# Linear-attention values as 512-column products by token tile, placed first among the side products

## The reference

```
h = RMSNorm(x);  P = h @ w_in
A = sparse attention(P): compressed blocks, selected blocks, sliding window
B = gated linear attention(P): q_b, k_b (256 columns each), v_b (512 columns), r_b, decay gate
x += (sigmoid(gA) * (A @ w_pa) + sigmoid(gB) * (B @ w_pb)) @ w_out
x += (gelu(dwconv3(h2 @ w_u)) * (h2 @ w_g)) @ w_down,   h2 = RMSNorm(x)
```

## Time and profile before

| | us |
|---|---|
| median of 3 runs (2158.03 to 2160.08) | 2159.13 |
| the profiled execution, its own time | 2148.94 |
| its span, first to last instruction | 2147.2 |
| PE busy | 2107.1 (98%) |
| DVE busy | 1144.9 (53%) |

### The profile page before, as it was taken

One profiled execution on the slowest core, in us unless ns is written; L12 is line 12 of the kernel. 1 busy time (PEld: TensorE's weight loads), 2 busy tenths in 40 slices (PEclk: granted clock), 3 DMA queues, 4 the chain that ended last, 5 costly groups with the idle time before them and its releaser, 6 DMA issues.

```text
span 2147.2 us, 30516 instructions
## 1 busy us (share of the span) xinstructions
PE 2107.1 (98%) x11911; PEld 1687.4 (79%) x11911; DVE 1144.9 (53%) x2384; ACT 516.2 (24%) x1108; POOL 675.8 (31%) x789
## 2 busy tenths in 40 slices
PE   8999989999999999999999999999999999999999
PEld 7787866678888888888887877666788888888887
DVE  5566746755337455453336666567453454555522
ACT  3124124532112222210122232244221222222000
POOL 5240042204223444434331400621232234444332
PEclk9999999999999999999999999999999999999999
DMA  5874631113222222222284736201132222222222
GB/s 155 273 236 181 248 118 40 41 43 101 79 82 79 79 79 89 90 79 74 68 291 120 267 136 273 81 28 32 59 104 82 79 79 79 79 89 91 79 69 75
DMA packets 172305, 237.53 MB, mean 111 GB/s; under 512 B 39551, under 2 KB 151680, under 8 KB 169408
## 3 DMA queue, kind: packets, MB, share of 16 engines
q1 hardware_dynamic: 153320, 133.11, 20.6%
q0 software_dynamic: 18400, 102.36, 12.8%
q10 hardware_dynamic: 444, 0.12, 0.0%
HBM read 222.76 MB, written 21.11 MB: 114 GB/s over the span
## 4 chain that ended last, share of the span: by engine, by line
PE 91%; DVE 2%; ACT 2%; POOL 2%; DMA 2%; issue 1%; SPq 0%; POOLq 0%; DVEq 0%; ACTq 0%
PE PS L1005 52%; PE PS L948 10%; PE PS L1163 6%; PE PS L970 5%; PE PS L996 3%; PE PS L1499 2%; PE PS L1416 2%; PE PS L460 2%; PE PS L1427 2%; DMA arena<-in_cache_kv_slc_dram,idx 2%; ACT arena L1710 1%; POOL arena L835 1%; PE PS L1374 1%; PE PS L1399 1%; PE PS L1548 1%
## 5 line engine op out<-in xcount | busy, mean ns | idle before, releaser
L1005 PE MATMUL PS<-arena,ring 128*128 128x272 f32 x1632 | 401.3, 393 | 0.9 <-DVE xT L2076 0.6
L1005 PEld LDWEIGHTS PS<-arena,ring 128*128 128x128 f32 x1632 | 309.3, 190 | 65.9 <-issue 2.4
L1710 ACT ACTIVATE arena<-PS 128x272 f32<-128x272 f32 (+12 forms) x442 | 176.1, 423 | 739.6 <-PE PS L1005 286.4
L2076 DVE TENSOR_TENSOR arena<-PS,arena 128x272 f32<-128x272 f32 (+4 forms) x298 | 138.7, 476 | 370.8 <-PE PS L1005 279.4
L1005 PE MATMUL PS<-hT,ring 128*128 128x272 f32 x1120 | 282.3, 397 | 5.9 <-DVE arena L2076 4.7
L1005 PEld LDWEIGHTS PS<-hT,ring 128*128 128x128 f32 x1120 | 213.6, 192 | 52.8 <-DVE arena L2076 5.2
L2076 DVE TENSOR_TENSOR xT<-PS,xT 128x272 f32<-128x272 f32 x224 | 99.0, 442 | 252.2 <-PE PS L1005 251.9
L862 POOL TENSOR_TENSOR qT<-ring 128x512 f32<-128x512 f32 (+1 forms) x38 | 48.8, 1284 | 384.7 <-PE PS L1005 255.7
L2082 DVE SCALAR_TENSOR_TENSOR arena<-arena,prm 128x32 f32<-128x32 f32 (+1 forms) x176 | 143.8, 817 | 22.1 <-ACT arena L1710 18.2
L948 PE MATMUL PS<-hT,ring 128*128 128x272 f32 x640 | 150.7, 394 | 2.3 <-DVE small L2373 1.5
L1005 PE MATMUL PS<-arena,kv_kT 128*128 128x272 f32 x616 | 149.7, 392 | 0.0
(11 more groups left out here) (362 smaller groups left out, 2989.7 us busy)
## 6 DMA issues: line engine op xcount, KB each, us to landing
ring<-in_w_up_dram SPq DMA_DIRECT2D x88, 512.0 KB, 4.6
ring<-in_w_in_dram SPq DMA_DIRECT2D x68, 512.0 KB, 4.8
ring<-in_w_down_dram SPq DMA_DIRECT2D x32, 512.0 KB, 4.4
arena<-in_state_kv_win_dram POOLq DMA_DIRECT2D x4, 2048.0 KB, 8.3
ring<-in_w_out_dram SPq DMA_DIRECT2D x16, 512.0 KB, 4.3
out_dram<-in_state_kv_win_dram POOLq DMA_DIRECT2D x2, 4064.0 KB, 39.6
ring<-in_w_down_dram SPq DMA_DIRECT2D x16, 384.0 KB, 3.5
ring<-in_w_in_dram SPq DMA_DIRECT2D x16, 256.0 KB, 4.6
```

Source lines behind the costliest of these rows:

```text
L1005: mm = pe.matmul(PS[:, bank, 0:HALF], weight[:, k, :], rhs(k), start=(start and k == 0), stop=(stop and k == kc - 1), skip_group_check=not ...
L1710: return nc.scalar.activation(out, in_, func, **kw)
L2076: return nc.vector.tensor_tensor(out, a, b_, op)
```

## The change

The four value tiles become one product each over all 512 columns (both halves of `v_b`, two ring slots, as one moving operand), and stand first: tiles 0 and 1 at the compression, tile 2 at `("s",0,3)`, the sampled tokens' product and tile 3 at `("s",0,2)`. `qb0`, `qb1` and `kb0` move behind, and `kb1` is split by token halves over `("b",1)` and `("b",2)`. The weights are loaded in the new order.

```diff
-    steps = ["q0", "q1", "kv1", "kv2", "kv0", "gl", "qb", "kb", "vb0", "vb1", "rb0", "rb1"]
+    steps = ["q0", "q1", "kv1", "kv2", "kv0", "gl", "vb0", "vb1", "qb", "kb", "rb0", "rb1"]
...
-    at = {("s", 0, 5): ("vb00",), ("s", 0, 4): ("vb01",), ("s", 0, 3): ("qb0",), ("s", 0, 2): ("qb1",), ("s", 0, 1): ("kb0",), ("s", 0, 0): ("kb1",),
-          ("b", 0): ("vb0b", "vb0h"), ("b", 1): ("vb1l",), ("b", 2): ("vb1h", "vb1b"), ("s", 1, 0): ("rb00",), ("u", 0): ("rb01",)}
+    at = {("s", 0, 5): ("vb0",), ("s", 0, 4): ("vb1",), ("s", 0, 3): ("vb2",), ("s", 0, 2): ("vbf3", "vb3"), ("s", 0, 1): ("qb0",),
+          ("s", 0, 0): ("qb1",), ("b", 0): ("kb0",), ("b", 1): ("kb1l",), ("b", 2): ("kb1h",), ("s", 1, 0): ("rb00",), ("u", 0): ("rb01",)}
...
+            def wide_few(ticket, names):
+                w = wide_weights(names)
+                pe.wait_ge(*S.claim(pe, "T", ticket))
+                b = S.banks(pe, ticket)
+                for k in range(KC):
+                    q = NS * (k % 4)
+                    mm = pe.matmul(PS[q:q + NS, b, :].rearrange("p (j n) -> p j n", j=2), hT[:, k, SEQ:NT], w[:, :, k, :], start=(k < 4), stop=(k >= 4))
+                mm.then_inc(*S.fill(pe, ticket))
+            def wide_tiles(ticket, names, tiles, pool="T"):
+                w = wide_weights(names)
+                pe.wait_ge(*S.claim(pe, pool, ticket))
+                b = S.banks(pe, ticket)
+                for j, t in enumerate(tiles):
+                    for k in range(KC):
+                        mm = pe.matmul(PS[:, b + j, :].rearrange("p (j n) -> p j n", j=2), hT[:, k, P * t:P * t + P], w[:, :, k, :], start=(k == 0), stop=(k == KC - 1))
+                mm.then_inc(*S.fill(pe, ticket))
...
+                        if name[-1] in "lh":
+                            a = "lh".index(name[-1])
+                            w = ring[:, s, :].rearrange("p (k n) -> p k n", n=WCOLS)
+                            pe.wait_ge(*S.claim(pe, pool, name))
+                            b = S.banks(pe, name)
+                            half_product(b, w[:, :, P * int(name[2]):P * int(name[2]) + P], lambda k: hT[:, k, HALF * a:HALF * a + HALF], KC, True, True).then_inc(*S.fill(pe, name))
...
+                            move = copy(vbs if name == "vbf3" else vT[:, int(name[2]), :], PS[:, b, :])
+                        elif name[-1] in "lh":
+                            a = "lh".index(name[-1])
+                            move = copy(kbT[:, int(name[2]), HALF * a:HALF * a + HALF], PS[:, b, 0:HALF])
```

More of the change, by code:

```diff
@@ L241, in last_ticket @@
     if name[0] in "qkvr" and name[:2] != "kv":
-        return {"q0": "q1", "q1": "q3", "vb0": "vb0h", "vb1": "vb1b"}.get(name, name + "1")
+        return {"q0": "q1", "q1": "q3", "vb0": "vb3", "vb1": "vb3", "kb": "kb1h"}.get(name, name + "1")
     if name[:2] == "kv":
@@ L616, in _ @@
                             (dst[:, :, 24:40], w_in[one, :, O_LR:O_LR + 16].rearrange("o (k p) n -> p (o k) n", p=P))])
-                for name, c0 in (("qb", O_QB), ("kb", O_KB), ("vb0", O_VB), ("vb1", O_VB + 256), ("rb0", O_RB), ("rb1", O_RB + 256)):
+                for name, c0 in (("vb0", O_VB), ("vb1", O_VB + 256), ("qb", O_QB), ("kb", O_KB), ("rb0", O_RB), ("rb1", O_RB + 256)):
                     cols_of(name, w_in, c0)
@@ L981, in few, with wide_weights @@
                 mm.then_inc(*S.fill(pe, ticket))
+            def wide_weights(names):
+                for name in names:
+                    pe.wait_ge(*w_landed(pe, name))
+                s0, s1 = sorted(wslot(name)[0] for name in names)
+                return ring[:, s0:s1 + 1:s1 - s0, :].rearrange("p j (k n) -> p j k n", n=WCOLS)
+            def wide_few(ticket, names):
[14 more added lines that the diff above has]
+                mm.then_inc(*S.fill(pe, ticket))
             def raw_products(tickets, slot, norm, mean_at, raw0, total):
@@ L1186, in side @@
                             continue
-                        s = wload(name[:-1])
+                        if name == "vbf3":
+                            wide_few(name, ("vb0", "vb1"))
+                            continue
                         if name[:2] == "vb":
-                            if name[3] == "b":
-                                few(name, s, 256)
-                            else:
-                                tm(name, s, 0, 256, 256, {"0": (0,), "1": (1,), "l": (0, 1), "h": (2, 3)}[name[3]])
+                            wide_tiles(name, ("vb0", "vb1"), (int(name[2]),), pool)
+                            continue
+                        s = wload(name[:2] if name[:2] in ("qb", "kb") else name[:-1])
+                        if name[-1] in "lh":
[4 more added lines that the diff above has]
+                            half_product(b, w[:, :, P * int(name[2]):P * int(name[2]) + P], lambda k: hT[:, k, HALF * a:HALF * a + HALF], KC, True, True).then_inc(*S.fill(pe, name))
                         else:
@@ L1327, in small_values @@
                     b = S.banks(pe, "vbf")
-                    for name in ("vb0b", "vb1b"):
-                        pe.wait_ge(*S.drained(pe, name))
+                    pe.wait_ge(*S.drained(pe, "vbf3"))
                     pe.matmul(PS[0:NS, b, :], fold4[:, :], vbs, start=True, stop=True).then_inc(*S.fill(pe, "vbf"))
@@ L2321, in side_copy @@
                             dv.wait_ge(*S.at(dv, "x_stored"))
-                            cc = slice(256 * int(name[2]), 256 * int(name[2]) + 256)
-                            if name[3] == "b":
-                                move = copy(vbs[:, cc], PS[:, b, 0:256])
-                            else:
-                                t0, t1 = {"0": (0, 1), "1": (1, 2), "l": (0, 2), "h": (2, 4)}[name[3]]
-                                move = copy(vT[:, t0:t1, cc], PS[:, b, 0:256 * (t1 - t0)].rearrange("p (t n) -> p t n", n=256))
+                            move = copy(vbs if name == "vbf3" else vT[:, int(name[2]), :], PS[:, b, :])
+                        elif name[-1] in "lh":
+                            a = "lh".index(name[-1])
+                            move = copy(kbT[:, int(name[2]), HALF * a:HALF * a + HALF], PS[:, b, 0:HALF])
                         else:
@@ L2643, in decay_step @@
                     if step == "q":
-                        for name in ("qb0", "qb1", "kb0", "kb1"):
+                        for name in ("qb0", "qb1", "kb0", "kb1l", "kb1h"):
                             dv.wait_ge(*S.drained(dv, name))
```

## The result

| | before | changed | ratio, 95% interval |
|---|---|---|---|
| the pair that was predicted, median us | 2159.39 (4 runs) | 2199.91 (2198.03 to 2201.53, 4 runs) | 1.0188 (1.0171 to 1.0206) |
| timed again later, median us | 2160.23 (15 runs) | 2200.98 (2199.80 to 2203.56, 5 runs) | 1.0185 (1.0171 to 1.0199) |
| span of the profiled execution, us | 2147.2 | 2199.8 | |

The changed kernel is slower by 1.9%, 40.5 us. The forecast was 2200.1 us.

What follows compares the result with a forecast made beforehand. PE, busy 98% of the span, was taken as the bound. Terms sum to +20.5 us a layer, +41.0 for two, on 2148.94 giving 2189.9, plus 10.2 between profiled execution and median: 2200.1 us, range 2184 to 2209.

Steps and rivals of the forecast that it cites:

- value tiles at the compression: At two early places a tile grows from 3.5 to 7.0 us with no wait to cover it: +7.0 us a layer.
- `("s",0,3)`: At this sample step a query product of 7.54 us becomes a value tile of 7.0: -0.5 us a layer.
- `("s",0,2)` to the key scores: From this step to the key scores: +10.7 us a layer, 9.1 of it PE's waits, the rest work.
- block region: First turn of probabilities to second key scores: 28.6 us, only -2.0 a layer, since gathers and DVE hid the rest.
- clock: Passes behind long PE waits run slow at 1.2 GHz: 1.8 us per wait on average, +5.3 us a layer.
- The wide pass: In the value tiles, one pass of 512 columns takes 0.438 us, twice a 256-column pass, so the form gains nothing visible.
- The bank waits: PE waits for DVE to drain banks: 3.3 us ahead of tile 3, 5.8 us ahead of qb0.
- The rival without bank waits: Drains at ("s",0,2) come in time, so only 1.5 us of work is added there: 2174.7 us in all; chance 0.06.
- Three stands a layer: PE waits of 3.3 us before tile 3, 5.8 before qb0, over 3 before the last key turn, each losing clock.
- the two named causes: What ends the block region: DVE's order of copies, turns and softmax (+27.6), or a late third gather (+28.9).
- The one with the block region giving nothing back: Gathers last as long, a copy stands in their way: +2.0 us a layer, one more stand, about 2207; chance 0.04.
- the no-slower case: Early side work replaces idle time if ow1 is drained early, compression hides a wait, gathers end sooner: about 2158; chance 0.03.

Runs made afterwards that it cites:

- e4: Changed kernel with each value tile as two products of 256 columns, 128 passes a layer for 64: 2191.52 us, 1.0194 of the kernel before.
- e1: Changed kernel with DVE's copies of the sampled tokens' product and tile 3 moved ahead of block_add(0) and two key turns: 2175.50 us, 1.0129 of before.
- e2: Changed kernel with tile 3 ahead of the sampled tokens' product at the same place: 2179.35 us, 1.0143 of the kernel before.
- e3: Changed kernel with both moves, DVE's copies ahead of block_add(0) and tile 3 ahead of the sampled tokens' product: 2162.97 us, 1.0067 of before.
- e6: Changed kernel with unread products laid into two waits, 7 ahead of tile 3 and 12 ahead of qb0: 2180.35 us, 1.0149 of before.
- e7: Changed kernel with the second four key gathers cut to 64 of 128 rows each: 2194.84 us, one run.
- e9: Changed kernel's wide tiles at the last four samples' steps, qb0 at ("s",0,0), qb1, kb0 and whole kb1 in the block region: 2150.84 us, 1.0012 of before.
- e10: The changed kernel itself, timed again beside the kernel before: 2200.98 us, 1.0185 of before.
- e12: Changed kernel with e3's two moves and e8's filler move: 2169.82 us, 1.0046 of the kernel before.
- e11: e9 with e8's filler move: 2160.64 us, 1.0000 of the kernel before.
- e8: Kernel before with filler product f1 moved from step 3 to step 4 of the prompt attention: 2142.52 us, 0.9974 of before.

## Why the prediction was right

Terms in us a layer, each from the rows of the changed kernel against those of before.

| term | predicted | layer 1 | layer 2 |
|---|---|---|---|
| value tiles at the compression, `("s",0,5)` and `("s",0,4)` | +7.0 | +6.8 | +6.8 |
| `("s",0,3)` | -0.5 | -0.5 | -0.5 |
| `("s",0,2)` to the key scores, without the clock | +10.7 | +11.0 | +11.0 |
| block region, at full clock | -2.0 | -1.8 | -2.2 |
| clock | +5.3 | +6.9 | +5.5 |
| sum | +20.5 | +22.4 | +20.6 |

- **The wide pass.** Taken as 0.438 us; 16 of them hold PE 6.92 us, which is 0.433 each. e4 shows that the form is free, to 0.04 us a tile.
- **The bank waits.** 3.3 and 5.8 us predicted, 3.75 and 5.82 measured, with the releasers that were named: DVE's sum of `ow1` and the 128x512 copy. The first is 0.45 longer; 0.2 of it is that the sampled tokens' product took 1.90 us where 2.1 was counted. e1 and e2 removed each on its own, e3 both, and the time fell by their rows. The rival without bank waits is out.
- **The clock.** Three stands a layer at an average 1.8. Measured: 1.72, 2.53 and 2.65 in layer 1, 1.72, 2.37 and 1.43 in layer 2 (8.80 - 7.08, 10.13 - 7.60, 7.11 - 4.46; 8.80 - 7.08, 9.97 - 7.60, 5.89 - 4.46). For these three stands the mechanism was right, and the term a little small (5.3 a layer for a mean of 6.2): it took its average from 16 passes behind 2.37 and 3.92 us, and both the 32 passes behind 5.82 us and, in layer 1, the key scores behind 3.39 and 1.25 us lost more. The signs named passes at twice their length; that held for a part of each product only (8.80 for 7.08, not 14), as in the rows that the average came from. e6 confirms the mechanism by taking the clock loss away with the waits unchanged. The bound that the prediction drew, a loss from 2.37 us of waiting on and none under it, did not hold in the other runs (last section).
- **The block region.** 28.6 us predicted, 28.81 and 28.25 measured, with DVE's turn as the releaser of the last wait. Which of the two named causes sets how much is shown by the traces under e7: DVE's order 27.7 us, the third gather the rest. e9 agrees (7.5 us more work for 0.7 us). The weights ahead of the gathers freed them little, if it was they: the third tile could be turned 20.2 us into the region for 20.4 before, in layer 2 19.6 for 20.3.
- **The total.** Both layers sum to 43.0 us. The profiled spans differ by 52.6: 7.4 more are a slow stretch at 64 to 75 us that is no part of the change, and 2.2 lie in small differences elsewhere. The medians differ by 40.5, and e4, in the set where before takes 2148, is 43.6 above it. In that set the sum fits within 1 us; in the pair that was predicted it is 2.5 too large, and part of the agreement of 2200.1 with 2199.9 is the luck of a clock term 0.9 us a layer too small. What gives the 2.5 us back there stays open.
- **The 10.2 us between profiled execution and median.** I added them as a constant without a cause. e10 to e12 give part of one (below).

No rival was needed. The one with the block region giving nothing back was wrong by the rows, and of the conditions of the no-slower case none was met: `ow1` was summed too late for tile 3, the tiles at the compression cost their whole 6.8 us, and the gathers ended late enough to hold DVE's third turn by 1.14 us (DVE's timeline of the changed kernel, 288.93). Another placement nearly reaches its time: e9.

## What to carry to other kernels

A product that is twice as long costs nothing for its form and everything for its place: ask at each place which bank it claims, who had that bank before it, and what the draining engine has queued ahead of that drain; here moving one copy up and swapping two tickets took back 28.6 of 43.6 us (e3 and e4, one set). A place that hides work behind another engine must be kept filled: emptying it gives a wait, and the wait then costs the clock as well. Price a wait of TensorE like those of 3.7 us and more here as its length plus 1.5 to 3.1 us of slow passes behind it, unless another wait stands just behind, which absorbs them; between 0.6 and 2.4 us these runs show both the loss and none.

## What the runs showed of the hardware that I had not expected

**A slow stretch that comes and goes with the set of runs.** PE's timeline at 64 to 69 us of the changed kernel run again, and then of the kernel before:

```profile
64.85 0.39 PE L948 MATMUL PS<-kbT,mean_h 128*128 128x272 f32 x1 [1.71 <-issue]
66.25 0.39 PE L948 MATMUL PS<-kbT,mean_h 128*128 128x272 f32 x1 [1.01 <-issue]
```

```profile
63.43 2.00 PE L948 MATMUL PS<-kbT,mean_h 128*128 128x272 f32 x8
```

In e10 PE stands 1 us or more between single passes, for nothing that the profile names, and its granted clock falls to 0.50 in 68 to 72 us. All DMA engines are busy there (share 1.05) in both kernels. The stretch is in all four traces taken where the kernel before has a median near 2160 us (the changed kernel's, e10, e11, e12) and in none of the nine taken elsewhere: before, profiled at 2148.94, and e1 to e9, where its median is 2148. It is thus no effect of the change: e1 to e4 load the same weights in the same order and show none. The record names a different chip for each of the three later sets (0, 2 and 13) and none for the pair that was predicted, so chip and set can't be told apart. The kernel before was not traced in a 2160 set; if it has the stretch there too, it accounts for some 7 of the 10 to 12 us between these sets. A ratio within one set is then nearly free of it, a difference across sets is not. What PE waits for isn't shown.

**The clock doesn't go by the length of the last wait.** Behind waits of 1.22 and 0.57 us the 16 passes of `kb1h` took 3.91 us in layer 1 of the changed kernel and 3.90 in that of e2, but 5.49 in e1 and e6 and 6.96 in e3; in layer 2 of these same three programs they took 3.90. Behind 1.65 to 1.68 us 16 passes took 5.59 in both layers of e8 and in layer 2 of e11, and 3.90 in layer 1 of e11 and both layers of e12. Behind the old wait of 2.37 us they took 5.4 to 5.6 in the kernel before and the changed one, and 3.93 in layer 2 of e8 and of e12 and in both layers of e11. The same waits cost nothing or up to 3 us. Behind 3.7 us and more there was a loss every time, of 1.5 to 3.1 us. The Trainium skill, in "TensorE: Matmul & The Clock Gate" under "A second HAM failure mode: psum-queue depth-cycling", says that short stops between groups of matmuls that cycle through banks can make the clock oscillate. The prediction gave that rule nothing for waits under 2.37 us. Layer 1 of e1, e3 and e6 agrees with the rule; their layer 2, the changed kernel and e2 do not. What decides between them stays open.

**Halved gathers are not faster.** With 64 rows of 128 each, the third of four gathers was usable 17.1 us after its issue, for 16.8 with all rows, and the 16 DMA engines were just as busy (1.05 and 1.03) at half the rate (213 and 442 GB/s). Why isn't shown.
